# Routing a mixture of experts from half rows: the layer norm folded into the router weights, the first pass's tokens picked by a one-hot product

## The reference, cut to what matters

```python
x = layer_norm(ALPHA * x + merged @ w_out, ln1_g, ln1_b)
scores = sigmoid(x @ router_w)                      # 32 experts, 4 groups of 8
sel = scores + router_b
group_score = sum of the best two sel in each group
grp = argmax(group_score)
expert = the best two experts of that group, by sel
gate = scores[expert] / sum(scores[expert])
moe_out[token] = sum over its two experts of gate * (silu(x @ w_gate[e]) * (x @ w_up[e])) @ w_down[e]
out = layer_norm(ALPHA * x + moe_out, ln2_g, ln2_b)
```

## Time and profile before

| | |
|---|---|
| median of 3 runs | 1109.42 us (1108.97 to 1109.49) |
| the profiled execution: its own time | 1111.02 us |
| its span, first to last instruction | 1109.3 us |
| PE busy | 993.4 us (90%) |
| DVE, ACT, POOL busy | 469.6, 279.3, 219.2 us |
| mean granted PE clock | 0.972 |
| bytes moved by DMA | 256.68 MB |

### The profile page before, as it was taken

One profiled execution on the slowest core, in us unless ns is written; L12 is line 12 of the kernel. 1 busy time (PEld: TensorE's weight loads), 2 busy tenths in 40 slices (PEclk: granted clock), 3 DMA queues, 4 the chain that ended last, 5 costly groups with the idle time before them and its releaser, 6 DMA issues.

```text
span 1109.3 us, 16552 instructions
## 1 busy us (share of the span) xinstructions
PE 993.4 (90%) x6068; PEld 464.9 (42%) x6069; DVE 469.6 (42%) x1006; ACT 279.3 (25%) x461; POOL 219.2 (20%) x331
## 2 busy tenths in 40 slices
PE   7999999999999999999994588889888888888774
PEld 3644465466457447444454233333333333332221
DVE  0695542563373363422336134433344444442333
ACT  1123312321322232200001023333333333332331
POOL 3000010010010010033000123333333333343332
PEclk9999999999999999999995599999999999999998
DMA  9332211210220220473709599999999999999992
GB/s 274 121 78 73 58 40 40 71 44 21 76 55 24 57 58 2 154 271 136 320 35 399 167 400 415 397 411 416 417 416 415 415 416 416 415 415 415 419 397 87
DMA packets 93855, 256.68 MB, mean 231 GB/s; under 512 B 15444, under 2 KB 60500, under 8 KB 68976
## 3 DMA queue, kind: packets, MB, share of 16 engines
q1 hardware_dynamic: 81904, 240.54, 56.3%
q0 software_dynamic: 11104, 13.29, 3.4%
q10 hardware_dynamic: 800, 2.15, 0.5%
HBM read 260.90 MB, written 21.23 MB: 254 GB/s over the span
## 4 chain that ended last, share of the span: by engine, by line
PE 52%; DMA 14%; SPq 12%; DVE 8%; issue 8%; POOL 4%; ACT 1%; POOLq 1%; DVEq 0%; ACTq 0%
PE proj L1282 11%; SPq L461 11%; PE proj L1241 11%; DMA y_rows<-const,raw 8%; PE proj L1462 5%; PE bank L1372 5%; PE bank L1450 5%; PE bank L1533 3%; DMA xT_sb<-w_gu 3%; DMA out<-raw 2%; PE bank L1554 1%; PE proj L1249 1%; POOL pass_sb L528 1%; POOL const L544 1%; PE proj L1260 1%
## 5 line engine op out<-in xcount | busy, mean ns | idle before, releaser
L1282 PE MATMUL proj<-xT_sb,ring 128*128 128x512 f32 x384 | 182.1, 607 | 0.0
L1533 PE MATMUL bank<-arena 128*64 128x512 f32 x544 | 122.1, 596 | 16.2 <-PE bank L1554 9.5
L1167 DVE TENSOR_TENSOR raw<-bank,const 128x512 f32<-128x512 f32 x33 | 22.8, 691 | 242.4 <-DMA out<-raw 242.3
L1241 PE MATMUL proj<-xT_sb,ring 128*128 128x512 f32 (+1 forms) x272 | 119.1, 594 | 0.0
L1282 PEld LDWEIGHTS proj<-xT_sb,ring 128*128 128x128 f32 x384 | 68.3, 189 | 68.3 <-issue 64.8
L1533 PEld LDWEIGHTS bank<-arena 128*64 128x64 f32 x544 | 43.0, 137 | 95.1 <-issue 82.8
L1241 PEld LDWEIGHTS proj<-xT_sb,ring 128*128 128x128 f32 (+1 forms) x272 | 50.7, 188 | 64.6 <-issue 64.5
L1533 PE MATMUL bank<-gates,arena 128*64 128x512 f32 x256 | 60.2, 622 | 8.4 <-PE bank L1554 4.8
L752 ACT ACTIVATE pass_sb<-bank 128x256 f32<-128x256 f32 x33 | 12.7, 383 | 201.1 <-PE bank L1533 201.1
L1372 PEld LDWEIGHTS bank<-arena 64*64 64x64 f32 x1536 | 52.8, 134 | 18.2 <-ACT arena L703 9.1
L499 POOL MEMSET arena<- 64x64 f32 x8 | 1.2, 145 | 291.7 <-DVE arena L923 257.9
(11 more groups left out here) (278 smaller groups left out, 1349.6 us busy)
## 6 DMA issues: line engine op xcount, KB each, us to landing
arena<-w_gu SPq DMA_DIRECT2D x64, 1024.0 KB, 22.4
gates<-w_gu SPq DMA_DIRECT2D x32, 1024.0 KB, 20.8
arena<-w_down SPq DMA_DIRECT2D x24, 1024.0 KB, 23.1
ring<-w_in SPq DMA_DIRECT2D x42, 512.0 KB, 3.9
gates<-w_down SPq DMA_DIRECT2D x16, 1024.0 KB, 22.7
branches<-w_down SPq DMA_DIRECT2D x16, 1024.0 KB, 25.6
xT_sb<-w_gu SPq DMA_DIRECT2D x16, 1024.0 KB, 24.9
ring<-w_gu SPq DMA_DIRECT2D x16, 1024.0 KB, 24.4
```

Source lines behind the costliest of these rows:

```text
L1241: ins = pe.matmul(proj[0:w, b, :], ring[:, slot, k, 0:w], xT_sb[:, k, :], start=(k == 0), stop=(k == KT - 1))
L1282: ins = pe.matmul(proj[:, gate_at["bank"], :], ring[:, gate_at["slot"], k, :], xT_sb[:, k, :], start=(k == 0), stop=(k == KT - 1))
L1533: ins = pe.matmul(bank[SLOTS * h:SLOTS * h + SLOTS, 0, :], xeT[:, k % 4, SLOTS * (k // 4):SLOTS * (k // 4) + SLOTS], gu[k // 2][:, k % 2, ...
```

## The change

The layer norm's gain and offset go into the router's weights, once: row d of `router_w` is multiplied by ln1_g[d], the column sums of that give a mean to be subtracted, those of `router_w` times ln1_b a constant to be added. So the router can be fed with the raw residual, and the row's deviation is applied to the 32 logits. Gains and offsets come as columns (`ln_cols`: two loads of 1024 single values each, on SP's queue ahead of `w_out`). `mix` goes over the four groups' first half rows and then their second ones, and each half row is turned and routed as it comes (4 transposes, 4 router products). ACT scales x1's rows in place, POOL multiplies by the gain and adds the offset. `w_out` is loaded in two halves, and SP's order of the first loads is new. The best two experts of a row come from one MAX8 for each group of tokens. Expert 0's first 64 tokens are picked out of x1 on the chip by a one-hot product of PE, and so pass 0 waits for no gather and not for the tables; the gathers begin with pass 1. `keep_clock` are PE products whose result nobody reads, after marked DVE steps. Passes 32 and 33 run in the form of the others, not in their own. Some semaphores are merged. The diff, cut to its core:

```diff
+        ln_cols = sb("ln_cols", [P, 2, KT])
-        wout_sb = cut(KT * D, r="p (k n) -> p k n", k=dict(k=KT))
-        merged = cut(KT * T, r="p (k t) -> p k t", k=dict(k=KT))
+        wout_sb = cut(KT * D, r="p (i k n) -> p i k n", k=dict(i=2, k=KT))
+        merged = cut(KT * T, r="p (c k t) -> p c k t", k=dict(c=TT, k=KT))
...
         @block.sync
-            sp.dma_start(wout_sb, w_out.rearrange("(k p) n -> p k n", p=P)).then_inc(s_wout, 16)
+            for i in range(2):
+                sp.dma_start(ln_cols[:, i, :], rows[:, 2 * SGU + D * i:2 * SGU + D * i + D].rearrange("a (k p) -> p (a k)", p=P),
+                             allow_slow_non_contiguous=True).then_inc(s_rw, 16)
+            for i in range(2):
+                sp.dma_start(wout_sb[:, i, :, :], w_out.rearrange("(k p) n -> p k n", p=P)[:, :, T * i:T * i + T]).then_inc(s_wout, 16)
...
-            sp.wait_ge(s_mx, 2 * TT)
-            for c in range(NCH):
-                load(1, c, 1)
+            for done, freed in ((TT, (0, 1)), (TT + 2, (4,)), (2 * TT, (2, 3, 5))):
+                sp.wait_ge(s_mx, done)
+                for c in freed:
+                    load(1, c, 1)
+            sp.wait_ge(s_routed, 2 * TT)
+            load(3, 3, 3)
             sp.wait_ge(s_x1, TT)
             load(3, 2, 3)
-            sp.wait_ge(s_scp, 1)
-            load(3, 3, 3)
             sp.wait_ge(s_x1st, 16 * TT)
+            sp.wait_ge(s_onehot, 1)
             for c in (0, 1):
                 load(3, c, 3)
...
         @block.gpsimd
+            pool.wait_ge(s_lnrows, 16)
+            for c in range(TT):
+                pool.wait_ge(s_xhat, c + 1)
+                pool.tensor_tensor(x1[:, c, :], x1[:, c, :], ln_rows[:, 0, :], MUL).then_inc(s_pool, 1)
+                pool.wait_ge(s_pool, KT + c + 1)
+                pool.tensor_tensor(x1[:, c, :], x1[:, c, :], ln_rows[:, 1, :], ADD).then_inc(s_x1, 1)
...
         @block.scalar
+            for n in range(TT):
+                turned_out(n)
+            for c in range(TT - 1):
+                row_root(c)
+                turned_out(TT + c)
+                row_scaled(c)
+                if c:
+                    row_stored(c - 1)
+            turned_out(2 * TT - 1)
+            row_root(TT - 1)
+            act.activation(warm[:, 1:2], warm[:, 0:1], ACT.Sigmoid)
+            act.wait_ge(s_logit, 1)
+            act.activation(scores[:, :, :], scores[:, :, :], ACT.Sigmoid).then_inc(s_score, 1)
+            row_scaled(TT - 1)
+            row_stored(TT - 2)
+            row_stored(TT - 1)
+            act.wait_ge(s_xe0, 1)
+            act.wait_ge(s_onehot, 1)
+            act.activation(xe, bank[:, 0, :], ACT.Copy).then_inc(s_firstxe, 1)
...
-            with act.If(more > 0):
-                with act.Fori(0, more) as i:
+            for n in range(2):
+                with act.If(more > n):
+                    one_pass(N_EXP + n, n)
+            with act.If(more > 2):
+                with act.Fori(2, more) as i:
                     one_pass(i + N_EXP, None)
...
         @block.vector
+            def residual(i, c):
+                n = TT * i + c
+                dve.wait_ge(s_mx, n + 1)
+                part = x1[:, c, T * i:T * i + T]
+                dve.scalar_tensor_tensor(part, part, ALPHA, proj[:, n % 2, :], MUL, ADD).then_inc(s_pre, 1)
+                dve.wait_ge(s_pre, n + 1)
+                then(dve.bn_stats(ln_stat[:, c, 6 * i:6 * i + 6], part))
...
-                then(dve.tensor_scalar(x1[:, c, :], x1[:, c, :], ln_mv[:, c, 0:1], ln_rs[:, c:c + 1], SUB, MUL))
-                then(dve.tensor_tensor(x1[:, c, :], x1[:, c, :], ln_rows[:, 0, :], MUL))
-                dve.tensor_tensor(x1[:, c, :], x1[:, c, :], ln_rows[:, 1, :], ADD).then_inc(s_x1, 1)
+                dve.scalar_tensor_tensor(half_rs[:, c:c + 1], ln_mv[:, c, 0:1], -1.0, ln_rs[:, c:c + 1], MUL, MUL).then_inc(s_shift, 1)
...
+            dve.wait_ge(s_routed, 2 * TT)
+            for c in range(TT):
+                ins = dve.scalar_tensor_tensor(scores[:, c, :], bank[:, 4, c * N_EXP:(c + 1) * N_EXP], ln_rs[:, c:c + 1], bw_sb[:, :], MUL, ADD)
+            ins.then_inc(s_logit, 1)
...
-            then(dve.tensor_tensor(sel_g, sel_g, grp[:, 2, :].unsqueeze(2).broadcast_to([P, NG, PER_GROUP]), MUL))
...
+            for c in range(TT):
+                ins = dve.max(top8[:, c, :], sel[:, c, :])
+            then(ins)
+            marks.append(seq["n"])
             for k in range(TOPK):
-                then(dve.tensor_reduce(best, sel[:, :, :], AX_X, MAX))
-                then(dve.tensor_tensor(pick, sel[:, :, :], best.unsqueeze(2).broadcast_to([P, TT, N_EXP]), ALU.is_equal))
-                then(dve.tensor_tensor(pick, pick, bc("expert_left", TT), MUL))
+                for c in range(TT):
+                    ins = dve.scalar_tensor_tensor(pick[:, c, :], sel[:, c, :], top8[:, c, k:k + 1], C("expert_left"), ALU.is_equal, MUL)
+                then(ins)
...
             dve.wait_ge(s_rank, 1)
+            for c in range(TT):
+                dve.tensor_scalar(first_hot[:, c, :], C("slot_iota")[:, 0:SLOTS], rank_ps[:, c, 0:1], chosen[:, 1 + c, 0:1],
+                                  ALU.is_equal, MUL).then_inc(s_firsthot, 1)
...
+            turned(0)
             dve.wait_ge(s_tabp, 1)
...
         @block.tensor
+            for n in range(2 * TT):
+                mix(n, 0)
+                if n == 1:
+                    pe.wait_ge(s_m3, KT)
+                    pe.wait_ge(s_wfold, 1)
+                    pe.matmul(bank[:, 5, 0:2 * N_EXP], C("ones"), w_sums[:, :, :], start=True, stop=True).then_inc(s_wsump, 1)
+                if n:
+                    turn_half(n - 1)
+                mix(n, 1)
+                if n > 1:
+                    router_half(n - 2)
+            router_half(2 * TT - 2)
+            turn_half(2 * TT - 1)
+            router_half(2 * TT - 1)
+            def keep_clock(columns):
+                pe.matmul(proj[:, 0, 0:columns], C("ident"), const[:, 0:columns], start=True, stop=True)
+            for mark in marks:
+                pe.wait_ge(s_dve, mark)
+                keep_clock(3 * P)
             pe.wait_ge(s_chosen, 1)
...
+            pe.wait_ge(s_x1, TT)
+            for c in range(TT):
+                pe.wait_ge(s_firsthot, c + 1)
+                for h in range(2):
+                    ins = pe.matmul(bank[SLOTS * h:SLOTS * h + SLOTS, 0, :], first_hot[:, c, :], x1[:, c, T * h:T * h + T],
+                                    start=(c == 0), stop=(c == TT - 1))
+            ins.then_inc(s_onehot, 1)
+            turn(0, first=True)
...
-            pe.wait_ge(s_tab, 1)
-            turn(0)
             pe.wait_ge(s_first, 1)
```

More of the change, by code:

```diff
@@ L1211, in _ @@
             more = dve.value_load(more_i[0:1, 0:1], min_val=0, max_val=MORE)
-            with dve.If(more > 0):
-                with dve.Fori(0, more) as i:
+            for n in range(2):
+                with dve.If(more > n):
+                    products(N_EXP + n)
+                    normed(N_EXP + n - 1)
+                    finish(N_EXP + n, n)
+            with dve.If(more > 2):
+                with dve.Fori(2, more) as i:
                     products(i + N_EXP)
@@ L1483, in _, with mix @@
[L1483 to L1494 removed]
+            def mix(n, part):
+                i, c = divmod(n, TT)
+                if n >= 2 and part == 0:
+                    pe.wait_ge(s_pre, n - 1)
+                for k in range(4 * part, 4 * part + 4):
+                    if n == 0:
+                        pe.wait_ge(s_merged, k + 1)
+                    ins = pe.matmul(proj[:, n % 2, :], merged[:, c, k, :], wout_sb[:, i, k, :],
+                                    start=(k == 0), stop=(k == KT - 1))
+                if part:
+                    ins.then_inc(s_mx, 1)
```

211 lines of the change are left out of this document (110 added, 101 removed).

## The result

The changed kernel takes 1099.12 us in the median of 4 runs (1098.97 to 1099.46), the kernel before beside it 1109.45 (1108.97 to 1109.52): a ratio of 0.9908, 95% interval 0.9891 to 0.9925. It is faster, by 10.3 us and not by the 16.6 forecast, and 1099.12 lies just outside the range (1087 to 1099). The profiled execution has a span of 1097.1 us (its own time 1099.05), 12.2 less than that of before.

A forecast was written before the change was run, and what follows sets the result against it. DMA engines, full from 640 us, were taken as the bound, so an earlier stream start ends the kernel earlier. Stream start 12.7 + gaps 2.5 + last pass 1.4 = 16.6 us off the 1109.42 median: 1093 us, range 1087 to 1099.

The forecast's parts named there:

- Mix: Products with w_out, with half turns and half routings between them: end at 586.1 us instead of 582.1.
- MAX8: Start of the expert choice behind the router's logits: 591.4 us instead of 595.8.
- the hold on DVE: In the choice, POOL's two long products block two DVE steps, some 2.0 and 2.3 us.
- the choice: DVE's choice of experts: 6.35 us if nothing holds DVE, ending at 597.7; with POOL's blockades, 602.0 us.
- the one-hot product: PE's picking of pass 0's tokens: 3.7 us at full clock, done at 608.3 us; the gather's 9.0 us go.
- the two rivals on DVE and the clock: In the routing: DVE not held, 1088 us, chance 0.27; idle products don't hold PE's clock, 1097 us, chance 0.23.
- The small DVE products: In the choice, two bursts of four small DVE products: 0.47 us each burst, bounds 0.3 to 1.2.
- The column loads: Rival on SP's queue ahead of w_out: slow single-value loads delay mix; 1134 us at 40 us each, chance 0.03.
- What is late next: After the one-hot product, SP's queue bounds, not pass 0: stream starts at 621.9 us against 634.6, 12.7 us earlier.
- The prediction's own sign: DMA after the one-hot product: no idle engines from there, and 416 GB/s from 622 us.
- Gaps: Four slices from 638 to 749 us under 416 GB/s: 2.5 of 2.7 us of waiting for free places go.
- The last pass: Pass 32 in the common form: DVE's L1170 follows L1167 directly, 1.4 us earlier.

The follow-up runs named there:

- e3: Against the changed kernel, POOL's two norm products for the last row group wait until DVE's choice is done; 1099.31 us (before 1109.20).
- e4: Against the changed kernel, the five idle products on PE are left out; 1099.30 us (before 1109.20).
- e7: Against the changed kernel, DVE itself norms the last row group, without ACT's scaling and POOL's products; 1096.69 us (before 1109.20).
- e6: Against the changed kernel, only the last pass is put back in its own form; 1099.71 us (before 1108.72).
- e15: The changed kernel run again, untouched; 1099.88 us (before 1109.11).
- e16: The kernel before run again, untouched; median 1109.30 us.

## Why the prediction was wrong

*The routing: right.* Mix, MAX8, the hold on DVE, the choice and the one-hot product came within 0.3 us of the forecast, and the two rivals on DVE and the clock fell; e3 shows the hold, e4 that the idle products had a part in the clock. The small DVE products took 0.74 us for four where 0.47 were taken, within their bounds (0.3 to 1.2). That the one-hot product found the full clock was in part luck: the clock rose, fell and rose again on the way there, and in e3 and e7 the same product ran at half clock (6.50 and 6.54 us). The column loads landed 3.3 us after issue (row of the DMA issues: 4 KB each), for 2.4 in the nearest row, 38.6 us to spare: that rival fell too.

*What is late next: this failed.* "Pass 0's start is thus not the new bound (617 leaves 4.9 us to spare); the queue is." The queue is one bound, but its term was too large: 12.7 us forecast, 9.5 by the bytes left at 640 us. The step let the queue run from 608.3 us at 416 GB/s, with one start of 1.65 us, and had the stream begin at 621.9. That is 12.5 MB by 640 us ((640 - 609.95) x 416); 11.0 were moved (343 GB/s over 608 to 640 us), and the missing 1.5 MB are 3.6 us, near the 3.2 that the term was too large by. Two things that it put at nothing show in the windows. c4 and c5 did not follow c0 and c1 without a break, for the tables came 2 us late, behind a product at half clock. And from 620 to 628 us, busy all the time, the engines moved 374 and 333 GB/s beside the loads of norm rows and the gathers; the step charged these for their 0.75 MB alone. The prediction's own sign, 416 GB/s from 622 us and no idle engine from the one-hot product on, failed by this. What SP's first reload gained, 12.4 us, is close to the 12.7, but it counts an issue and not the bytes.

*Gaps: this failed too, and it held the clue.* The prediction read four slices under 416 GB/s and let 2.5 us of them go, "with passes further ahead of the stream"; 1.2 came (10.7 us to the last weights' products, less 9.5). The slice of 397 is where expert 9's load waits for pass 6; after the change it is 395. Had the prediction asked what SP waited for in it, it would have found the 14.4 us of waiting on PE's L1533. The passes are further ahead only if they gain more than the stream, and they gained about as much: 13.7 us at pass 0's start, less 2.1 from pass 0 to pass 1 and 1.4 from there to pass 6, 10.3. What was hidden before was the gather of pass 1: it ran beside pass 0, whose own gather had been waited for; now it is the first, cannot start before the tables, and PE waits 2.3 us for it in the middle of pass 0, loses the clock and runs the second half 2.4 us slower. The prediction costed the gather that went and not the one that took its place. But this was the smaller part of the miss: e3 and e4 had their passes 2.4 and 1.5 us further ahead, and with the same bytes left at 640 us their ends came within 0.5 us of the changed kernel's.

*The last pass: right*, 1.5 us for 1.4, and e6 gives the cause.

*The reference.* Of the profiled span the forecast was 16.6 and 12.2 came: 9.5 + 1.2 instead of 12.7 + 2.5, and 1.5. Of the medians only 10.3 came, and 9.2 in e15. The profiled execution of before was 1.6 us over its median; e16 shows one 3.5 us shorter, nearly all of it gained by pass 6.

What stays open: why passes 1 to 6 took 1.4 us more after the change (68.0 us in e15 agrees; the trace has it in pass 2, 14.6 us for 13.7, and pass 3, 14.0 for 13.4, where PE waits 0.82 and 0.63 us for the next gather instead of 0.40 and 0.23; no experiment was made on it), which transfers keep the busy engines under 416 GB/s from 620 to 628 us, and what brings PE's clock back or not in the 10 us after the choice.

## What to carry to other kernels

A stream of loads that looks full has two limits: the bytes left once it is at full rate, and the last load that waited for its place while the queue was empty. Reckon both before summing: the first from the bytes moved and not from the issue of the first load, the second from every slice a few per cent under the full rate and what the queue's engine waited for in it. A gain in one counts only as far as the other follows. When a wait for a gather goes, cost the next gather that was hidden beside it. Keep GpSimd's long products of SBUF operands away from a chain of small DVE products: each can cost the length of GpSimd's instruction, 2.3 us for 8 columns here.

## What the runs showed of the hardware that was not expected

A gather of 64 rows issued 2 us earlier (615.15; 617.10) had its tokens turned at the same time (624.68; 624.63). PE's clock moved between its two levels (1.2 and 2.4 GHz) six times between 590 and 615 us, and what one product lost by it another had back: one-hot 3.65 and tables 3.82 us with idle products, 4.87 and 2.23 without, and the same time in the end. Two executions of one kernel can differ by 3.3 us up to the same load (711.06 and 714.32 us), while the time from there to the last weights' products repeats within 0.3 (373.4 and 373.7). Busy DMA engines need not move the full 416 GB/s: 374 and 333 from 620 to 628 us, at busy shares of 1.01 and 1.06.
